# The forget bias of an attention head folded into its score product, in a hybrid encoder kernel on one core

## The reference, cut to what matters

```python
q = rms_norm(a_q.reshape(bsz, L, FOX_HEADS, FOX_HEAD_DIM), fox_q_gain[l])
k = rms_norm(a_k.reshape(bsz, L, FOX_HEADS, FOX_HEAD_DIM), fox_k_gain[l])
...
c = jnp.cumsum(jax.nn.log_sigmoid(f_logit.astype(jnp.float32)), axis=1)
...
for blk in range(L // Q_BLOCK):
    qs, qe = blk * Q_BLOCK, (blk + 1) * Q_BLOCK
    s = jnp.einsum('bhqd,bhkd->bhqk', qf[:, :, qs:qe], kf[:, :, :qe]) * scale
    s = s + c[:, :, qs:qe, None] - c[:, :, None, :qe]
    mask = jnp.arange(qs, qe)[:, None] >= jnp.arange(qe)[None, :]
    p = jax.nn.softmax(jnp.where(mask, s, -jnp.inf), axis=-1)
    outs.append(jnp.einsum('bhqk,bhkd->bhqd', p, vf[:, :, :qe]))
```

## Time and profile before

| | us |
|---|---|
| median of 3 executions | 1032.58 (1032.25 to 1032.63) |
| the profiled execution | 1033.05 |
| its span, first to last instruction | 1031.3 |
| TensorE busy | 1023.4 |
| VectorE busy | 680.3 |
| ScalarE busy | 523.5 |
| GpSimd busy | 205.0 |

### The profile page before, as it was taken

The page is one execution under the profiler, slowest core; times in us unless marked ns, Lnnn a source line. Parts: engine busy times, 40 slices in busy tenths (PEclk is TensorE's granted clock), DMA queues, the critical chain, the costliest instruction groups (busy, mean ns, idle before and its releaser), DMA issues.

```text
span 1031.3 us, 22763 instructions
## 1 busy us (share of the span) xinstructions
PE 1023.4 (99%) x9714; PEld 1006.2 (98%) x9714; DVE 680.3 (66%) x850; ACT 523.5 (51%) x628; POOL 205.0 (20%) x291
## 2 busy tenths in 40 slices
PE   8999999999999999999999999999999999999998
PEld 7999999999899999999999999999998999999998
DVE  7666656788668555555566665668987667555554
ACT  5645434565587534343475454436456765434341
POOL 0000899800002000000020019996000020000000
PEclk9999999999999999999999999999999999999999
DMA  8746454434325464545555555453442265464541
GB/s 301 269 158 209 164 200 162 162 128 161 124 83 204 164 209 164 202 164 200 176 205 207 181 186 204 163 204 123 153 138 92 92 228 204 164 203 163 203 163 42
DMA packets 26821, 178.44 MB, mean 173 GB/s; under 512 B 3121, under 2 KB 4161, under 8 KB 5761
## 3 DMA queue, kind: packets, MB, share of 16 engines
q1 hardware_dynamic: 25632, 173.03, 47.8%
q10 hardware_dynamic: 1008, 4.05, 1.1%
q0 software_dynamic: 112, 0.40, 0.1%
HBM read 176.42 MB, written 1.05 MB: 172 GB/s over the span
## 4 chain that ended last, share of the span: by engine, by line
PE 96%; DVE 2%; DMA 1%; SPq 0%; ACT 0%; issue 0%; DVEq 0%; ACTq 0%
PE ps L815 30%; PE ps L816 30%; PE ps L817 30%; DMA raw<-stream 1%; PE ps L968 1%; PE ps L1021 1%; PE ps L1086 1%; DVE lo L1228 0%; DVE in_lo L1427 0%; PE ps L1082 0%; SPq L363 0%; PE ps L1043 0%; ACT hi L577 0%; PE ps L1062 0%; PE ps L1031 0%; PE ps L1149 0%
## 5 line engine op out<-in xcount | busy, mean ns | idle before, releaser
L1228 DVE TENSOR_TENSOR lo<-raw,hi 128x2048 fp32r<-128x2048 f32 x130 | 302.7, 2337 | 200.0 <-ACT hi L577 199.9
L815 PE MATMUL ps<-xg_hi,hi 128*128 128x256 f32 x1408 | 399.3, 284 | 2.3 <-DVE lo L1311 1.4
L816 PE MATMUL ps<-xg_lo,hi 128*128 128x256 f32 x1408 | 398.4, 283 | 0.0
L817 PE MATMUL ps<-xg_hi,lo 128*128 128x256 f32 x1408 | 398.4, 283 | 0.0
L577 ACT ACTIVATE hi<-raw 128x2048 fp32r<-128x2048 f32 x130 | 247.1, 1909 | 176.4 <-PE ps L817 170.8
L815 PEld LDWEIGHTS ps<-xg_hi,hi 128*128 128x128 f32 x1408 | 270.3, 192 | 2.9 <-issue 2.8
L816 PEld LDWEIGHTS ps<-xg_lo,hi 128*128 128x128 f32 x1408 | 270.3, 192 | 0.1
L817 PEld LDWEIGHTS ps<-xg_hi,lo 128*128 128x128 f32 x1408 | 270.3, 192 | 0.0
L815 PE MATMUL ps<-act_hi,hi 128*128 128x256 f32 x704 | 199.4, 283 | 0.6 <-DVE act_lo L1266 0.6
L816 PE MATMUL ps<-act_lo,hi 128*128 128x256 f32 x704 | 199.2, 283 | 0.0
L817 PE MATMUL ps<-act_hi,lo 128*128 128x256 f32 x704 | 199.2, 283 | 0.0
(11 more groups left out here) (317 smaller groups left out, 1339.0 us busy)
## 6 DMA issues: line engine op xcount, KB each, us to landing
raw<-stream SPq DMA_DIRECT2D x160, 1024.0 KB, 4.9
par<-params ACTq DMA_DIRECT2D x2, 1463.0 KB, 9.1
raw<-stream SPq DMA_DIRECT2D x8, 256.0 KB, 7.3
rows<-stream SPq DMA_DIRECT2D x2, 1024.0 KB, 6.9
x<-xT ACTq DMA_DIRECT2D x4, 256.0 KB, 6.6
out<-x SPq DMA_DIRECT2D x8, 128.0 KB, 2.0
con<-consts POOLq DMA_DIRECT2D x1, 371.5 KB, 6.6
mask<-masks POOLq DMA_DIRECT2D x1, 20.0 KB, 6.7
```

Of the source, the lines that this page charges most:

```text
L815: pe.matmul(acc, w_hi, a_hi, start=start, stop=False, skip_group_check=True)
L816: pe.matmul(acc, w_hi, a_lo, start=False, stop=False, skip_group_check=True)
L817: return pe.matmul(acc, w_lo, a_hi, start=False, stop=stop, skip_group_check=True)
L1228: v.tensor_tensor(lo[slot][:, :], raw[slot][:, :], hi[slot][:, :].bitcast(F32), ALU.subtract).then_inc(lo_written, 1)
```

## The change

The queries and keys get a tile of their own for each head: `fqk` grows from two to four head slots, and a head keeps its 64 rows where they were (partitions 0 to 63 for even heads, 64 to 127 for odd ones). Eight further rows of each head's tile take the gates: partitions 64 to 71 for even heads, 0 to 7 for odd ones; partitions 8 to 63 of the odd heads are cleared by GpSimd once a layer. One product per head, over 72 or 128 rows, replaces the product and the outer product. The projected queries and keys go to `plain`, a view of the score buffer `sc`, and the normalization writes from there into `fqk`, for the even and the odd heads apart. The normalization of the keys stands further back in VectorE's order. The rows of `fl` and the constants that build them are rearranged accordingly.

```diff
-        fqk = sb("fqk", [P, 2, 2, T], F32, fox_mem)
+        fqk = sb("fqk", [P, 2, FOX_HEADS, T], F32, fox_mem)
...
-        fl = sb("fl", [GATES, 6, T], F32, fox_mem)
+        fl = sb("fl", [GATES, 3, T], F32, fox_mem)
...
+        plain = sc[:, :, :].rearrange("p h c -> p (h c)")[:, 0:4 * T].rearrange("p (w a t) -> p w a t", w=2, a=2)
...
                 sum_squares(l * 3 + 1)
+                pool.memset(fqk[0:64, :, 1:FOX_HEADS:2, :], 0.0).then_inc(heads_cleared, 1)
                 pool.memset(attn[:, :, :], 0.0).then_inc(attn_cleared, 1)
...
-                def fox_scores(t, first):
...
-                            pe.matmul(dst(hd), fqk[r:r + 64, 0, pair, tok], fqk[r:r + 64, 1, pair, 0:n],
-                                      start=True, stop=False, skip_group_check=True)
...
-                        last = pe.matmul(dst(hd), fl[:, 3, tok], fl[:, KEY_ROWS[hd], 0:n], start=False, stop=True,
-                                         skip_group_check=True)
...
+                def fox_scores(t, pair):
...
+                    for hd in (2 * pair, 2 * pair + 1):
+                        r = slice(0, GATES if hd % 2 == 0 else P)
+                        last = pe.matmul(bank(6 + hd % 2)[:, pair * n:(pair + 1) * n], fqk[r, 0, hd, tok],
+                                         fqk[r, 1, hd, 0:n], start=True, stop=True, skip_group_check=True)
+                    if pair == 1:
+                        last.then_inc(sc_done, 1)
...
-                project_tokens(9, {1: lambda: level(6), **fox_scores(1, 2)})
+                project_tokens(9, {1: lambda: level(6), 2: lambda: fox_scores(1, 0), 4: lambda: fox_scores(1, 1)})
                 level(7)
-                late_scores = fox_scores(0, 1)
-                project(10, {**late_scores, 4: lambda: (late_scores[4](), level(8))})
+                project(10, {1: lambda: fox_scores(0, 0), 3: lambda: fox_scores(0, 1), 4: lambda: level(8)})
...
-                v.tensor_scalar(fl[:, 3, :], cum, prm("query_rows", 0, 1)[0:GATES, :], prm("query_rows", 1, 1)[0:GATES, :],
-                                ALU.mult, ALU.add)
-                for hd in range(FOX_HEADS):
-                    last = v.tensor_scalar(fl[:, KEY_ROWS[hd], :], cum, prm("key_rows", 2 * hd, 1)[0:GATES, :],
-                                           prm("key_rows", 2 * hd + 1, 1)[0:GATES, :], ALU.mult, ALU.add)
+                v.wait_ge(heads_cleared, l + 1)
+                for odd in range(2):
+                    r = slice(0, 2 * FOX_HEADS) if odd else slice(64, GATES)
+                    v.tensor_scalar(fqk[r, 0, odd:FOX_HEADS:2, :], cum[r, :].unsqueeze(1).broadcast_to([2 * FOX_HEADS, 2, T]),
+                                    prm("query_rows", 0, 1)[r, :], prm("query_rows", 1, 1)[r, :], ALU.mult, ALU.add)
+                    for hd in (odd, odd + 2):
+                        last = v.tensor_scalar(fqk[r, 1, hd, :], cum[r, :], prm("key_rows", 2 * hd, 1)[r, :],
+                                               prm("key_rows", 2 * hd + 1, 1)[r, :], ALU.mult, ALU.add)
...
-                for w in range(2):
+                def normalize(w):
                     v.wait_ge(frn_ready, l * 2 + w + 1)
-                    t = fqk[:, w, :, :].rearrange("p a t -> p (a t)")
-                    v.scalar_tensor_tensor(t, t, fst[:, 0, 0:1] if w == 0 else prm("k_gain"), fsq[:, w, :],
-                                           ALU.mult, ALU.mult).then_inc(fqk_ready, 1)
+                    gain = fst[:, 0, 0:1] if w == 0 else prm("k_gain")
+                    for odd in range(2):
+                        r = slice(64 * odd, 64 * odd + 64)
+                        last = v.scalar_tensor_tensor(fqk[r, w, odd:FOX_HEADS:2, :], plain[r, w, :, :], gain[r, :],
+                                                      fsq[r, w, :].rearrange("p (a t) -> p a t", a=2),
+                                                      ALU.mult, ALU.mult)
+                    last.then_inc(fqk_ready, 1)
+
+                normalize(0)
                 scores(5)
                 extend(6)
                 split_in(4)
                 scores(6)
+                normalize(1)
```

More of the change, by code:

```diff
@@ L39 @@
 NC = T // LAG
-GATES = 64 + FOX_HEADS
+GATES = 64 + 2 * FOX_HEADS
 EPS = 1e-6
@@ L79 @@
 SMALL = [size for size in LEVELS if 2 * size <= BLK]
-KEY_ROWS = (4, 5, 0, 1)
 TWO_PI = 2.0 * np.pi
@@ L192, in build @@
         fox_mem = ExitStack()
-        fqk = sb("fqk", [P, 2, 2, T], F32, fox_mem)
+        fqk = sb("fqk", [P, 2, FOX_HEADS, T], F32, fox_mem)
         fv = sb("fv", [P, 2, 256], F32, fox_mem)
         fsq = sb("fsq", [P, 2, 2 * T], F32, fox_mem)
-        fl = sb("fl", [GATES, 6, T], F32, fox_mem)
+        fl = sb("fl", [GATES, 3, T], F32, fox_mem)
         sc = sb("sc", [P, FOX_HEADS, 384], F32, fox_mem)
         fox_mem.close()
-        sb("over_fox", [P, 6 * T])
+        sb("over_queries", [P, FOX_HEADS * T])
+        hgrn_hi = sb("hgrn_hi", [P, HEADS, T], F32R)
+        sb("over_values", [P, 2 * T])
         s5_hi, s5_lo = [sb(f"s5_{half}", [P, 2, T], F32R) for half in ("hi", "lo")]
         fox_hi, fox_lo = [sb(f"fox_{half}", [P, 2, T], F32R) for half in ("hi", "lo")]
-        hgrn_hi, hgrn_lo = [sb(f"hgrn_{half}", [P, HEADS, T], F32R) for half in ("hi", "lo")]
+        hgrn_lo = sb("hgrn_lo", [P, HEADS, T], F32R)
+        sb("over_scores", [P, T])
+        plain = sc[:, :, :].rearrange("p h c -> p (h c)")[:, 0:4 * T].rearrange("p (w a t) -> p w a t", w=2, a=2)
         y = trig_tmp[:, 0:4, :].rearrange("p (a b) t -> p a (b t)", a=2)
@@ L330, in build @@
         cum_ready = sem("cum_ready")
+        heads_cleared = sem("heads_cleared")
         sc_done = sem("sc_done")
@@ L720, in fox_norm @@
                     e.wait_ge(proj_dve, l * 9 + 6 + w)
-                    e.activation(fsq[:, w, :], fqk[:, w, :, :].rearrange("p a t -> p (a t)"), ACT.Square
+                    e.activation(fsq[:, w, :], plain[:, w, :, :].rearrange("p a t -> p (a t)"), ACT.Square
                                  ).then_inc(fsq_ready, 1)
@@ L1064, in s5_glu @@
                     last.then_inc(glu_done, 1)
-                def fox_scores(t, first):
+                def fox_scores(t, pair):
                     n, tok = (t + 1) * P, slice(t * P, (t + 1) * P)
[L1071 to L1081, removed]
-                            pe.matmul(dst(hd), fqk[r:r + 64, 0, pair, tok], fqk[r:r + 64, 1, pair, 0:n],
-                                      start=True, stop=False, skip_group_check=True)
-                    def sums(hd):
-                        last = pe.matmul(dst(hd), fl[:, 3, tok], fl[:, KEY_ROWS[hd], 0:n], start=False, stop=True,
-                                         skip_group_check=True)
[L1088 to L1093, removed]
+                    if pair == 0 and t == 1:
+                        pe.wait_ge(fqk_ready, l * 2 + 2)
+                        pe.wait_ge(cum_ready, l + 1)
+                        pe.wait_ge(frn_ready, l * 2 + 2)
+                    elif pair == 0:
+                        pe.wait_ge(sc_read, l * 2 + 1)
+                    for hd in (2 * pair, 2 * pair + 1):
[4 more added lines that the diff above has]
+                        last.then_inc(sc_done, 1)
                 def fox_transposes(t):
@@ L1575, in _ @@
                 cum = fl[:, 2, :]
-                v.tensor_scalar(fl[:, 3, :], cum, prm("query_rows", 0, 1)[0:GATES, :], prm("query_rows", 1, 1)[0:GATES, :],
-                                ALU.mult, ALU.add)
-                for hd in range(FOX_HEADS):
-                    last = v.tensor_scalar(fl[:, KEY_ROWS[hd], :], cum, prm("key_rows", 2 * hd, 1)[0:GATES, :],
-                                           prm("key_rows", 2 * hd + 1, 1)[0:GATES, :], ALU.mult, ALU.add)
+                v.wait_ge(heads_cleared, l + 1)
[6 more added lines that the diff above has]
+                                               prm("key_rows", 2 * hd + 1, 1)[r, :], ALU.mult, ALU.add)
                 last.then_inc(cum_ready, 1)
-                take(5, fqk[:, 0, :, :])
+                take(5, plain[:, 0, :, :])
                 split_in(4)
@@ L1586, in _ @@
                 scores(1)
-                take(6, fqk[:, 1, :, :])
+                take(6, plain[:, 1, :, :])
                 split_in(4)
@@ L1756, in _params @@
     put("k_gain", np.tile(inputs["fox_k_gain"][l], 2)[:, None])
-    rows = np.r_[0:FOX_HEADS, 64:64 + FOX_HEADS]
+    rows = np.r_[0:2 * FOX_HEADS, 64:GATES]
     bias, query, key = np.zeros((GATES, 1)), np.zeros((GATES, 2)), np.zeros((GATES, FOX_HEADS, 2))
[L1759 to L1762, removed]
+    bias[rows, 0] = np.tile(inputs["fox_f_bias"][l], 4)
+    for r in (0, 64):
+        query[r:r + FOX_HEADS, 0] = query[r + FOX_HEADS:r + 2 * FOX_HEADS, 1] = 1.0
+        for hd in range(FOX_HEADS):
+            key[r + hd, hd, 1], key[r + FOX_HEADS + hd, hd, 0] = 1.0, -1.0
     put("f_bias", bias)
@@ L1790, in _constants @@
     for j in range(FOX_HEADS):
-        gate_rows[j::BLK, j] = gate_rows[j::BLK, 64 + j] = 1.0
```

(1 more changed line is left out.)

## The result

| | before | changed |
|---|---|---|
| median of 6 executions, us | 1032.61 (1032.25 to 1033.03) | 1042.54 (1041.82 to 1042.98) |
| ratio of the executions | | 1.0094 (95%: 1.0083 to 1.0104) |
| the profiled execution, us | 1033.05 | 1042.70 |
| its span, us | 1031.3 | 1040.9 |
| mean granted clock of TensorE | 1.000 | 0.993 |

The change makes the kernel 0.94% slower, 9.9 us. The direction was forecast, and most of the mechanism. The forecast was 1039.6 us; the measured 1042.54 lies 0.9 us above the upper end of the range, 1041.6.

The account below looks back on a forecast made before the run. TensorE, busy 99% of the span without slack, bounds the kernel; per layer +5.2 (stall) - 2.9 (products) + 1.2 (clock) = +3.5 us, twice +7.0, taking 1033.05 to 1040.1, less 0.5 for the median: 1039.6 us, range 1036.4 to 1041.6.

Parts of the forecast that it names:

- Direction and mechanism: Slower, chance 0.96: TensorE waits for late keys at tile 2 of projection 9, once a layer, outweighing the products saved.
- The products: TensorE's head and outer products: new pairs 0.86 and 0.44 us, outer products 2.6 us; saving 2.9 us a layer.
- at the cost of one product: Alternative pricing of today's 64-row pairs as running side by side: saving only 1.3 us, time 3.2 us above the sum.
- The stall: TensorE at the first head product waits for normalized keys: 5.2 us a layer, between 4.9 and 5.5.
- The clock: TensorE's clock falls in the stall, so work behind it starts slow: 1.2 us a layer, between 0 and 1.6.
- The lower bound: Clock cost of 0 a layer, from the program's end, where a rest of 3.3 us still read 1.00.
- the case with no fall: Rival: stall as forecast but too short for the clock to fall; +4.6, so 1037.2 us; chance 0.30.
- The sum: Per layer +5.2 stall, -2.9 products, +1.2 clock: +3.5 us; twice, +7.0.
- The rows of the bias: VectorE's bias instructions take about 0.8 us more, hidden in its 3.2 us idle wait for TensorE at 255.39.
- GpSimd's clearing: New clearing of 64 x 1024 elements takes about 0.96 us, 38 us before VectorE asks for it, so hidden.
- The chain of masks and exponentials: Behind the stall, the mask starts 1.3 us later while TensorE is 3 us later, so the chain gains distance.
- VectorE's idle time before the mask: Behind the scores, this idle time was to go down from 3.4 to about 3.3 us.

Follow-up runs that it names:

- The first experiment: Changed kernel with the key normalization put back directly behind that of the queries: 1028.39 us, ratio to before 0.9954.
- the last experiment: Kernel before with its eight outer products a layer left out, so scores lack the forget bias: 1027.66 us, ratio 0.9953.
- The fifth experiment: Changed kernel with the key normalization after the second of the four splits: 1038.02 us, ratio 1.0053.
- the sixth experiment: Changed kernel with keys directly behind the queries and the later half's scores one tile later on TensorE: 1027.95 us, ratio 0.9953.
- the three profiles with falls: Changed kernel, 1042.54 us; kernel before with keys behind `scores(6)`, 1045.24 us; changed kernel with keys after the second split, 1038.02 us (medians).
- one program with a rest of 2.0 us: Changed kernel with the key normalization between `extend(6)` and the four splits: 1032.65 us, ratio 1.0000, executions from 1031.30 to 1036.10.

## Why the prediction was wrong, point by point

**Direction and mechanism: right.** TensorE waits for the keys, once a layer, at the first head product, because the two instructions stand behind the splits and the copies. The first experiment shows it by undoing this and nothing else.

**The products: right.** Forecast were 0.86 and 0.44 us for the new pairs, measured 0.87 and 0.44. The outer products cost 2.5 us a layer by the last experiment, 2.6 forecast. Taking the pairs of half height at what their rows said, drain included, and not at the cost of one product, was right too: at the cost of one product a pair, the changed kernel with early keys would have gained 2 x (1.3 - 0.5) = 1.6 us, and it gained 4.5. The Trainium skill ("TensorEngine Tiling (Array Packing)", "Tiling Modes") says that a change of mode drains the array. The 0.4 us that a pair of half height costs beyond one product agree with that; no run here tells a drain from another fixed cost of the pair.

**The stall: 5.45 for 5.2 us, a term sized a little too small.** What fell short is "I give each half the full price, a step of 0.66 us". The price of a half was right, 0.745 us, as for the whole; its step was not. The two halves do not overlap: 1.50 us for two, and the next instruction at a distance of 1.57. The 0.66 came from two instructions that both begin at partition 0, where the halves begin at 0 and 64. The bias rows of the changed kernel, eight at partitions 64 to 71 first and then eight at 0 to 7, show the same difference:

```profile
246.04 0.73 DVE L1572 TENSOR_SCALAR fqk<-fl,par 8x256 f32<-8x256 f32 x2
246.79 0.53 DVE L1569 TENSOR_SCALAR fqk<-fl,par 8x512 f32<-8x512 f32 x1
247.25 0.72 DVE L1572 TENSOR_SCALAR fqk<-fl,par 8x256 f32<-8x256 f32 x2
```

On the same partitions the next instruction begins 0.07 us before the end of the one ahead (247.25 against 246.79 + 0.53); at the change from 64 to 0 it begins 0.02 us behind it (246.79 against 246.04 + 0.73). No experiment varied this alone. The keys were ready at 279.62 for the 279.35 forecast: 0.11 is this in the keys themselves, 0.16 their later start (278.11 for 277.95). The chain between came out to the tenth (splits at 274.83 for 274.76, copies at 277.24 for 277.17). The stall stayed in its bounds, 4.9 to 5.5.

**The clock: 2.0 and 2.8 for 1.2 us, and outside its bounds. This broke the range.** The failed step is "For the new stall the cost is therefore between 0 and 1.6 us a layer", drawn from "The slow pace ran from 1.47 to somewhere between 3.3 and 4.7 us, a loss of half of 1.9 to 3.2". I took the slow stretch at the start of one execution as the longest that there could be. Twice in the changed kernel the clock stayed low for 6.8 us from its fall, and for 4.0 and 5.6 us after TensorE was back at work. Even the start itself is not the same from one execution to the next. The same 18 warm-up matmuls (ns min/median/max, first and last start), before and with the change:

```profile
L901 PE MATMUL ps<-in_hi x18: 387/397/795, 1.5 to 6.8; 128*128 128x512 f32 x18
L905 PE MATMUL ps<-in_hi x18: 387/632/796, 1.5 to 8.2; 128*128 128x512 f32 x18
```

In the first the slow ones, of 0.63 us, end with the start at 3.8 us; in the second with the start at 6.8, so they go on for more than 5 us. The start told how fast TensorE is at the low level; it bounded nothing in its duration. Nor does the granted clock tell it there: it reads 1.00 from the first microsecond in both profiles, though the starts are 0.43 us apart, so a 1.00 is to be trusted only where the pace of matmuls confirms it. The lower bound rested on such a reading, the tail of the earlier trace rows, where no matmul runs, and was also one instance: in another kernel the fall came after 1.9 us.

The rule of the Trainium skill ("TensorE: Matmul & The Clock Gate", "HAM oscillation — how this bites in real kernels"), that a burst behind a wait starts slow, holds here at each of the changed kernel's two waits, 0.50 in the rows; by it alone the case with no fall should have had less than the 0.30 that I gave it. The fifth experiment limits it: in its layer 2 the burst starts at full pace and the clock falls 1.7 us later.

**The sum.** Forecast 5.2 - 2.9 + 1.2 = +3.5 a layer, measured +4.6 and +5.4. Of the 2.9 us between 7.0 and 9.9, 0.5 are the stall and 2.4 the clock.

**What should hide did.** The rows of the bias took 0.7 us longer up to the next instruction (247.89 against 247.19), for the 0.8 forecast, and vanished in VectorE's idle time before 255.34; GpSimd's clearing is nowhere waited for. The chain of masks and exponentials gained distance behind the stall, as forecast, and came into view in the sixth experiment, where there is no stall. But the forecast that VectorE's idle time before the mask would go from 3.4 to about 3.3 us was wrong: it is 5.40, and the mask starts at 285.01, 3.6 us later than before and not 1.3. Its sum took the second pair of scores at the full pace, without the clock that the same prediction charged.

## What to carry to other kernels

Where one engine has no idle time, look first in a change for what its in-order partners now do before the operand that it needs: here one call of 1.5 us, put behind 4.8 us of work that was less urgent, cost nearly three times what the rewrite saved (15.7 us against 5.8). A rest of TensorE costs its length and often a stretch at half clock as well: here 1.7 to 3.2 us each in the three profiles with falls, at rests of 3.2 to 5.3 us, and nothing to 4.7 us for two rests of 2.0. Give such a term bounds from several executions, and never from one instance. And if such a wait can't be taken away, products that nobody reads inside it can pay: they brought back 4.3 us.

## What the runs showed of the hardware that I had not expected

- In the three profiles with falls, the clock fell 2.5, 4.1, 4.0, 2.7 and 1.9 us into a rest of TensorE, and once 1.7 us after a rest of 3.2 us was over; in one program with a rest of 2.0 us it fell in six of ten executions. The length of the rest alone does not decide it; what else does was not settled here.
- Having fallen, it stayed at the low level for 6.8 us in five of these six places, and for 3.4 us in the sixth. In the changed kernel TensorE worked in the last 4.0 and 5.6 us of that without a pause.
- At the start of the program the last slow matmul begins 2.3 us after the first in one profile and 5.3 us in another, while the granted clock reads 1.00 throughout.
- One VectorE instruction of 512 columns took 0.745 us on 64 partitions as on 128. Two in a row that begin at partitions 0 and 64 took 1.50 us together, where two that both begin at 0 start 0.66 us apart: a halved partition range gives nothing back, and the pair does not overlap.
